# Adding the squares of the pre-norms on GpSimd, with two tiles left for TensorE to sum

## The reference, cut to what matters

```
def rmsnorm(x, g):
    return x * rsqrt(mean(x * x, axis=-1) + eps) * g

x = x + 0.5 * rmsnorm(swiglu(rmsnorm(x, ffn1_pre_g)), ffn1_post_g)
x = x +       rmsnorm(token_mix(rmsnorm(x, mix_pre_g)), mix_post_g)
x = x + 0.5 * rmsnorm(swiglu(rmsnorm(x, ffn2_pre_g)), ffn2_post_g)
```

## Time and profile before

| what | us |
|---|---|
| median of 3 runs | 2019.62 (2019.52 to 2020.6) |
| the profiled execution | 2017.47 |
| its span | 2015.7 |
| TensorE busy with matmuls | 1969.7 (98%) |
| VectorE busy | 1286.0 (64%) |
| ScalarE busy | 779.5 (39%) |
| GpSimd busy | 84.5 (4%) |

### The profile page before, as it was taken

How to read it: one execution, slowest core, us unless ns; L and a number is a source line. 1 busy time by engine, 2 the same in 40 slices (tenths; PEclk the granted TensorE clock), 3 DMA queues, 4 the chain that set the end, 5 groups by cost and what they waited for, 6 DMA issues and landing times.

```text
span 2015.7 us, 36703 instructions
## 1 busy us (share of the span) xinstructions
PE 1969.7 (98%) x15320; PEld 1774.0 (88%) x15320; DVE 1286.0 (64%) x1997; ACT 779.5 (39%) x932; POOL 84.5 (4%) x164
## 2 busy tenths in 40 slices
PE   6999999999999999999999999999999999999998
PEld 6999988777777898999999999987776778999998
DVE  5776477666468676665377754866664677666644
ACT  5444354323332344333354544623324223443332
POOL 1111000000000000000011100000000000000000
PEclk9999999999999999999999999999999999999999
DMA  6888533333333443444458874334443334434442
GB/s 245 309 295 281 181 129 95 134 124 131 137 110 126 147 147 105 147 146 165 166 192 301 304 250 167 110 113 138 138 137 118 117 125 147 140 125 146 146 165 92
DMA packets 60844, 327.04 MB, mean 162 GB/s; under 512 B 7248, under 2 KB 7440, under 8 KB 34480
## 3 DMA queue, kind: packets, MB, share of 16 engines
q1 hardware_dynamic: 43200, 262.98, 37.9%
q0 software_dynamic: 17520, 62.27, 8.6%
HBM read 290.87 MB, written 34.36 MB: 161 GB/s over the span
## 4 chain that ended last, share of the span: by engine, by line
PE 92%; DVE 4%; ACT 1%; DVEq 1%; DMA 1%; issue 1%; SPq 0%
PE dps L707 46%; PE dps L611 11%; PE dps L561 11%; PE dps L646 9%; PE mx L761 7%; PE mx L945 1%; PE mx L663 1%; PE dps L634 1%; DMA raw<-in_wstream 1%; PE mx L1000 1%; PE mx L977 1%; DVE tmp L1816 1%; DVE rs L1507 1%; PE mx L561 1%; DVEq L1547 1%
## 5 line engine op out<-in xcount | busy, mean ns | idle before, releaser
L1077 ACT ACTIVATE whi<-raw 128x2048 fp32r<-128x2048 f32 (+1 forms) x144 | 269.1, 1869 | 487.8 <-PE dps L707 469.5
L707 PE MATMUL dps<-uh,whi 128*128 128x320 f32 x1408 | 430.2, 306 | 19.8 <-DVE wlo L1446 15.2
L1446 DVE TENSOR_TENSOR wlo<-raw,whi 128x2048 fp32r<-128x2048 f32 x136 | 311.7, 2292 | 209.0 <-ACT whi L1077 203.9
L707 PE MATMUL dps<-uh,wlo 128*128 128x320 f32 x1408 | 434.2, 308 | 0.0
L707 PE MATMUL dps<-ul,whi 128*128 128x320 f32 x1408 | 432.8, 307 | 0.0
L707 PEld LDWEIGHTS dps<-uh,whi 128*128 128x128 f32 x1408 | 264.8, 188 | 25.3 <-issue 18.6
L707 PEld LDWEIGHTS dps<-uh,wlo 128*128 128x128 f32 x1408 | 264.8, 188 | 0.0
L707 PEld LDWEIGHTS dps<-ul,whi 128*128 128x128 f32 x1408 | 264.0, 187 | 0.6
L611 PE MATMUL dps<-u,raw 128*128 128x320 f32 x768 | 234.8, 442 | 0.0
L707 PE MATMUL dps<-hfh,whi 128*128 128x320 f32 x704 | 220.4, 313 | 0.0
L707 PE MATMUL dps<-hfh,wlo 128*128 128x320 f32 x704 | 217.6, 309 | 0.0
(11 more groups left out here) (299 smaller groups left out, 3145.8 us busy)
## 6 DMA issues: line engine op xcount, KB each, us to landing
raw<-in_wstream SPq DMA_DIRECT2D x198, 1024.0 KB, 4.8
u<-in_wstream POOLq DMA_DIRECT2D x44, 512.0 KB, 7.1
split_store<-wha POOLq DMA_DIRECT2D x44, 512.0 KB, 7.7
raw<-in_wstream SPq DMA_DIRECT2D x44, 512.0 KB, 4.1
parts<-split_store SPq DMA_DIRECT2D x44, 512.0 KB, 5.1
hs<-in_st_hgrn POOLq DMA_DIRECT2D x8, 512.0 KB, 5.6
out_o_hgrn<-hs POOLq DMA_DIRECT2D x8, 512.0 KB, 2.9
out_yT<-x SPq DMA_DIRECT2D x2, 1280.0 KB, 4.5
```

The source lines that it names most:

```text
L707: m = pe.matmul(dps[:, 2 * half + c, 0:T], w[:, k, c * P:(c + 1) * P], v[:, k0 + k, :], start=first and k == 0 and i == 0, stop=last and k ...
L1077: return nc.scalar.activation(out, in_, f, **kw)
L1446: return nc.vector.tensor_tensor(out, a, b, op)
```

## The change

GpSimd adds the tiles of squares ahead of the sum: once the second, third and fourth pair of tiles is there, it adds that pair onto the first pair in `u`, one add of 128x640 elements each, with a drain between. It does so at the start of a layer (ahead of the wait at L472), ahead of the wait for `pa_ready` (L496) and behind the last head's store. TensorE then waits for the new semaphore `pre_added` and sums two tiles in place of eight. In a feed-forward this sum stands behind the third tile product (c = 0, k = 2; nine matmuls) of the second block; ahead of the mixer it stands where the last of the four calls stood. The computed values are the same but for the order of the additions.

```
--- before.py
+++ after.py
@@ -316,7 +316,7 @@
 
 
         names = """ones_loaded const_loaded lg_loaded prm_loaded prm_ready sw_loaded shift_loaded lru_loaded ss_loaded hs_loaded
-        block_done full_done half_done half_hi half_lo branch_hi branch_lo merged_hi merged_lo x_new x_first uh_first u_first sq_ready sq_added sq_last first_done hi_ready lo_ready uh_ready sum_done rt_ready u_ready u_half u_full nh_ready nl_ready x_spilled x_back turn_done turn_hi presplit silu_ready h_ready
+        block_done full_done half_done half_hi half_lo branch_hi branch_lo merged_hi merged_lo x_new x_first uh_first u_first sq_ready pre_added sq_added sq_last first_done hi_ready lo_ready uh_ready sum_done rt_ready u_ready u_half u_full nh_ready nl_ready x_spilled x_back turn_done turn_hi presplit silu_ready h_ready
         lgexp_in lgexp_out zero_ready pa_ready lora_in_ready lora_act_ready lora_done lora_ready
         kk0_ready kksq_ready kn_done norm_ready rkr_ready rk_done rkv_ready cumm_ready gam_ready ve_ready
         e_ready abq_done abq_ready tok_done tok_ready ao_ready z_done z_ready tinv_done tinvt_done tinv_ready tinvt_ready
@@ -468,7 +468,17 @@
             def lay(t, l):
                 return t[bass.ds(l, 1)]
 
+            def add_pre_squares(l, idx):
+
+                for j in range(1, 4):
+                    pool.wait_ge(S["sq_ready"], l * 24 + (4 * idx + j + 1))
+                    if j > 1:
+                        pool.drain()
+                    m = nc.gpsimd.tensor_tensor(u[:, 0:2, :], u[:, 0:2, :], u[:, 2 * j:2 * j + 2, :], ALU.add)
+                m.then_inc(S["pre_added"], 1)
+
             for l in range(L):
+                add_pre_squares(l, 0)
                 pool.wait_ge(S["sum_done"], l * 6 + 1)
                 pool.dma_start(sw[:, :, :], lay(smallw, l).rearrange("a p k n -> (a p) k n"))\
                     .then_inc(S["sw_loaded"], 16)
@@ -493,6 +503,7 @@
                         if q:
                             pool.wait_ge(pre_stored[h], (l * len(order) + q) * 16)
                             pool.sem_inc(S["presplit"], 1)
+                add_pre_squares(l, 2)
                 pool.wait_ge(S["pa_ready"], l + 1)
                 nc.gpsimd.tensor_copy(shift_out[:, :, 0:1], pa[:, :, TP - 1:TP])
                 nc.gpsimd.tensor_copy(shift_out[:, :, 1:NB + 1],
@@ -533,6 +544,7 @@
                                    hsn[:, :, :]).then_inc(S["hs_stored"], 16)
                     pool.wait_ge(S["hs_stored"], n * 32 + 32)
                     pool.sem_inc(S["hs_free"], 1)
+                add_pre_squares(l, 4)
 
             pool.wait_ge(S["shift_stored"], 16 * L)
             pool.wait_ge(S["lru_stored"], 32 * L)
@@ -570,7 +582,6 @@
                     u_wait(l, 1, k)
                     for h in range(H_A):
                         product(mx[:, h, 0:T], h, k, 0, (uh, ul), k == 0, False)
-                pre_sum(l, 2, 0)
                 for j in range(1, 4):
                     u_wait(l, 1, 2 * j)
                     for h in range(H_A):
@@ -578,7 +589,7 @@
                             m = product(mx[:, h, 0:T], h, k, 0, (uh, ul), False, k == KD - 1)
                         if j == 3:
                             m.then_inc(S["half_done"], 1)
-                    pre_sum(l, 2, j)
+                pre_sum(l, 2)
 
             def half_tiles(l, h):
 
@@ -656,14 +667,12 @@
                 for _ in range(n):
                     pe.matmul(mx[:, 2, 0:2 * P], ident, cst[:, 0:2 * P], start=True, stop=True)
 
-            def pre_sum(l, idx, j):
-
-                pe.wait_ge(S["sq_ready"], l * 24 + (4 * idx + j + 1))
-                for k in (2 * j, 2 * j + 1):
-                    m = pe.matmul(mx[:, 3, 0:T], ones, u[:, k, :], start=k == 0, stop=k == KD - 1,
-                                  skip_group_check=True)
-                if j == 3:
-                    m.then_inc(S["sum_done"], 1)
+            def pre_sum(l, idx):
+
+                pe.wait_ge(S["pre_added"], l * 3 + (idx // 2 + 1))
+                for k in range(2):
+                    m = pe.matmul(mx[:, 3, 0:T], ones, u[:, k, :], start=k == 0, stop=k == 1, skip_group_check=True)
+                m.then_inc(S["sum_done"], 1)
 
             def added_sum(l, idx):
 
@@ -689,7 +698,7 @@
                 else:
                     pe.wait_ge(S["u_ready"], l * 12 + (4 * n + k // 2 + 1))
 
-            def split_tiles(s, kt, hi, lo_, half, first=True, last=True, k0=0, norm=None, ends=None):
+            def split_tiles(s, kt, hi, lo_, half, first=True, last=True, k0=0, norm=None, behind=None, ends=None):
 
                 wh, wl = (v[s][:, 0:kt * 256].rearrange("p (k n) -> p k n", k=kt) for v in (whi, wlo))
                 order = [(c, k, 0) for c in range(2) for k in range(kt)]
@@ -711,8 +720,8 @@
                         m.then_inc(S["block_done"], 1)
                     elif ends and k == kt - 1:
                         m.then_inc(S["first_done"], 1)
-                    if norm and c == 1 and k == 2 * j + 1:
-                        pre_sum(norm[0], 2 * norm[1], j)
+                    if behind and c == 0 and k == 2:
+                        pre_sum(*behind)
 
             def ffn(l, b, q, f):
                 def split_in(i, j):
@@ -722,7 +731,8 @@
                 for s in range(2):
                     split_in(0, s)
                     pair_wait(l, q // 2, s)
-                    split_tiles(s, KD, uh[:, :, :], ul[:, :, :], s, norm=None if s else (l, 2 * f))
+                    split_tiles(s, KD, uh[:, :, :], ul[:, :, :], s, norm=None if s else (l, 2 * f),
+                                behind=(l, 4 * f) if s else None)
                 with pe.Fori(1, KF // 2) as i:
                     for s in range(2):
                         split_in(i, s)
```

## The result

The changed kernel takes 2044.51 us (median of 4 runs, 2042.35 to 2048.34) against 2019.57 us before: **ratio 1.0127, 95% interval 1.0109 to 1.0146**, slower. The profiled execution took 2045.45 us, 28.0 more than that of before; its span is 2043.7 us. The forecast was 2033.8 us in 2018 to 2044, so the median lies half a microsecond above the range. The sign and the mechanism came as forecast; the size was missed, by 11 us in the medians and by 14 in the profiled executions (+27.9 at the last norm, where +14.2 was forecast).

What follows compares the result with a forecast made beforehand. TensorE was taken as the bound, but VectorE's pace at the five later borders. Holds of VectorE, 3 x 3.6 + 2 x 2.85 = 16.5, less 2.3 at the start, gave +14.2: 2033.8 us, range 2018 to 2044.

Steps and rivals of the forecast that it cites:

- +14.2: Whole kernel: us added by VectorE being held at five borders, less 2.3 at the start; chance of VectorE held 0.57.
- the root's lateness: Feed-forward norm: the root comes 1.75 us behind the sum's old end, starting the third block 0.9 us late per border.
- GpSimd first: Borders: add starts before the renewal of x and holds VectorE; third block +5.1 us, ahead of the mixer +2.8.
- Rivals 1 and 2: 1: VectorE isn't held, 2020.1 us, chance 0.28. 2: the sums' time comes back in full, 2000.2 us, chance 0.05.
- Rival 4: Adds slow, over 3.5 us, the sum waits for them, VectorE not held: 2030 us with 5 us adds, chance 0.05.
- The adds ... ahead of the mixer, 2.5 us: Ahead of the mixer, 268.23 to about 270.8: 2.5 us of add are hidden before TensorE asks for the sum.
- 2.85: Each of two mixer borders: us lost to VectorE being held, between 2.8 and 2.9 for the two engine orders.
- Middle: 3 x 3.6: Three later feed-forward borders: 3.6 us lost at each, the middle of the two engine orders.
- +5.1 and +2.1: Feed-forward border: lateness of the third block in us, with GpSimd starting first and with VectorE starting first.
- Rival 3, the clock: TensorE's clock falls to 1.2 GHz for the second block (7 us) at five borders: +35 us, about 2055, chance 0.05.
- The start, -2.3: Start of the program: shorter sums let the third block start at 32.5 in place of 34.8, 2.3 us saved.
- upper bound for the add, 2.4 us: Each GpSimd add: at most 2.4 us, from the copies with twice their slope; gives +33 us in all.

Runs made afterwards that it cites:

- E1: The changed kernel without the GpSimd adds, TensorE summing only the first two tiles of squares: 2022.05 us, ratio 1.002.
- E4: The kernel before, with only the last sum call moved behind the third product of the second block in the feed-forwards, no GpSimd work: 2024.37 us, ratio 1.003.
- E2: The kernel before with all its sums, plus the 18 GpSimd adds into a scratch tile nobody reads: 2033.42 us, ratio 1.0071.
- E12: The changed kernel, with the drain between adds replaced by a wait on the count of adds done: 2040.42 us, ratio 1.0107.
- E3: The changed kernel with three filler matmuls behind steps 0 to 2 of the five later borders: 2041.92 us, ratio 1.0126.
- E8: The changed kernel with eight one-column GpSimd memsets ahead of each group of adds but the first: 2056.67 us, ratio 1.0185.
- E7: The kernel before, with the adds and two-tile sum only for the program's first norm, directly behind its first block: 2015.24 us, ratio 0.998.
- E11: The changed kernel with one wait for all four pairs of squares ahead of the first add: 2050.53 us, ratio 1.0156.

## Why the prediction was wrong

**What was right.** That the sums' time comes back only at the start (E1). The length of the sum call and the root's lateness (1.75 against 1.76, E4). That VectorE is held, with GpSimd first, by lengthened renewals: steps of 4.20 us (3.8 to 4.2 forecast), waits for `ul` of 29.9 us (over 20). Rivals 1 and 2 fell with E2 and E1. Rival 4 fell as it was put, since an add takes 1.76 us and VectorE is held; but the sum does wait for the adds ahead of the mixers, for another reason.

**Where the 13.7 us between +14.2 and +27.9 came from:**

- *"The adds ... ahead of the mixer, 2.5 us" are hidden*: the step that failed. `drain` was costed at nothing, without a reason given; it takes 4.1 us there, so adds 2 and 3 end at 274.1, TensorE stands and its clock falls. 5.9 us by the ledger, removed by E12. With the drain gone the border costs 2.7, where the forecast had 2.85 (2.8 for GpSimd first).
- *"Middle: 3 x 3.6"*: both orders of the two engines were worked out for a feed-forward, +5.1 and +2.1, and their mean taken. The profile has GpSimd first at the first add of every border, and E3 shows 5.1, 5.3 and 5.1 us. Taking the mean cost 3 x 1.5 = 4.5 us. The order could have been seen: the squares that release the add end at 772.45 (771.73 + 0.72), before the renewal starts at 772.79. The agreement with 5.1 is partly luck: the three holds add up to 4.0 us as in that case (split_lo was put 4.2 late), and the moved sum to 1.1, but the add takes 1.76 us (1.3 forecast; 1.56 with little beside it) of which it holds VectorE for 1.4, and add 2 came late and held another instruction than was assumed.
- *Rival 3, the clock*: right that it falls, wrong as all or nothing. It fell in all five borders, for some 7 us each, but mostly where TensorE waits anyway. In the feed-forwards it cost 0.2, 0.1 and 2.1 us (changed against E3), not 7 each: 2.4 us. The last one differs because the slow stretch began later, at 1799.5, and so lay over the nine products and the sum that the root waits for, where in layer 0 it had ended at 789. The inverse came 5.40 us behind `wlo` there, 3.54 in layer 0. The clock belonged into the sum as a small term, not among the rivals at 35 us.
- *The start, -2.3*: -0.9 in this execution, 1.4 us of scatter, as the clock came up 3.1 us later; E1 and, up to the first mark, E8 show the forecast's value.
- The rest, -0.5 us, is the mixers' scatter (-0.3), a mixer border that costs 2.7 without the drain where 2.85 was forecast, and rounding.

The inverse of the last feed-forward's norm, beside that of layer 0 (792.01 [3.54], shown above):

```profile
1807.10 2.15 DVE L1517 RECIPROCAL rs<-rt 128x320 f32<-128x320 f32 x1 [5.40 <-ACT rt L1087]
```

The prediction's own upper bound for the add, 2.4 us, gave +33 and so 2052; the range left out its very end and stopped at 2044. A stall of GpSimd itself and a partly fallen clock had no part in it. The measured median lies half a microsecond outside; each of the first two terms above is many times that.

**What stays open.** Why the products of E8 are 2 ns longer each. What the drain does in its time (below). Why the slow stretch of the clock begins later in one border than in another.

## What to carry to other kernels

An engine with 4% of busy time is not free to use: ask whether it reads SBUF, and beside which VectorE instructions, and price each add at the time that it holds the other engine, here its length less 0.4 us, once for each overlap on the path. Moving work from TensorE pays only where TensorE sets the pace; do it there alone (E7), and count every synchronising instruction that comes with it, a drain above all, as work. Where two orders of two engines are worked out, find from the timeline which one it is rather than average them.

## What the runs showed of the hardware

**A drain on GpSimd takes time of its own.** The idle time that belongs to the first drain of a group was 0.34 us at the start, 2.37 in the second feed-forward's border and 4.09 ahead of the mixer, and repeated to about 0.02 us in each kernel with adds and drains where it could be read. By the code GpSimd had issued 2, 27 and 48 DMAs since the drain before, which makes 0.08 us for each ((2.37 - 0.34) / 25, (4.09 - 2.37) / 21). Ahead of the first feed-forward of layer 1 it had issued none since the drain before, and the second add started 2.53 us after the first had ended, against 2.44 without a drain (E12): 0.1 us. That the time depends on the number of DMAs is only a fit to these four points; no run changed the number. It is not a wait for those transfers: the code had waited for their stores long before (the adds ahead of the mixer follow 67 us of idle time). Nor is it the add before: in E11 the drain stands directly behind the add, in the changed kernel it begins 2.4 us after the add ended, and it takes some 4.1 us either way.

```profile
16.75 5.11 POOL L477 TENSOR_TENSOR u<-u 128x640 f32<-128x640 f32 x2 [0.34 <-issue]
```

**The hold works both ways.** Alone an add takes 1.56 us; beside VectorE 1.76, and at the start 2.4, behind a `wlo` that was running (12.69 to 14.98), and once 3.4, beside the next `wlo`:

```profile
14.00 2.41 POOL L477 TENSOR_TENSOR u<-u 128x640 f32<-128x640 f32 x1 [9.47 <-ACT u L1087]
```

**The clock fell in borders in which TensorE did its products alone and waited between the steps**, from its 2.4 to its 1.2 GHz level: in all five borders of the changed kernel, with waits of 1.7 and 2.2 us, and in three of E1, behind one wait of 1.7. The other two borders of E1 had the same wait and stayed at 1.00, so the waits alone do not decide it. It stayed at 1.00 in all borders of the profiled executions of E2, where the sums stood in the steps and the waits were 0.6 to 1.1 us, and of E3, where three filler matmuls stood behind steps 0 to 2 and the waits were 0.4 to 0.9. Ahead of the products that the path needs it cost about 1 us in each border of a mixer.
